# Seven half-size products for the mixing output projection of a hybrid encoder block, with its weight sums made earlier in the program

## What is computed

```
proj = rmsnorm(x) @ w_in            # columns for mLSTM, HGRN2 and the merge gates
y_m, y_h = mlstm(...), hgrn2(...)   # the HGRN2 values come from hg_i, token-major
merged = sigmoid(gate_m) * (y_m @ w_branch_m) + sigmoid(gate_h) * (y_h @ w_branch_h)
x = x + merged @ w_out              # the mixing output projection, 1024x1024 by 1024x1024
u = rmsnorm(x)
q_x = u @ w_q_x                     # cross attention follows, then the gated FFN
```

## Time and profile before

| what | value |
|---|---|
| median of 3 runs | 2567.12 us |
| the profiled execution, its own time | 2570.34 us |
| its span in the trace | 2568.6 us |
| granted TensorE clock, mean | 0.998 |
| PE busy | 2537.1 us (99%) |
| DVE, ACT, POOL busy | 1641.1 (64%), 914.6 (36%), 751.1 (29%) us |
| token-major HGRN projection on PE, first and last start | 478.5 to 565.3 us |
| mixing output projection on PE, with 5 transposes | 1562.42 to 1659.67 us |

### The profile page before, as it was taken

How to read it: one execution, slowest core, us unless ns; L and a number is a source line. 1 busy time by engine, 2 the same in 40 slices (tenths; PEclk the granted TensorE clock), 3 DMA queues, 4 the chain that set the end, 5 groups by cost and what they waited for, 6 DMA issues and landing times. The chain is left out here.

```text
span 2568.6 us, 35010 instructions
## 1 busy us (share of the span) xinstructions
PE 2537.1 (99%) x13888; PEld 2198.3 (86%) x13888; DVE 1641.1 (64%) x1839; ACT 914.6 (36%) x1123; POOL 751.1 (29%) x705
## 2 busy tenths in 40 slices
PE   7999999999999999999999999999999999999998
PEld 7888888889999999998888889977898888888887
DVE  5675555338887888866655424433447998887557
ACT  6342222133343333332324422333233443343433
POOL 2033223002111121235552001167412465553001
PEclk9999999999999999999999999999999999999999
DMA  8323333432323323344444536155414233335755
GB/s 284 117 79 125 106 100 130 136 120 92 103 98 108 103 98 115 107 141 159 159 141 160 168 123 213 34 180 194 159 34 147 74 123 116 106 107 181 280 195 180
DMA packets 184194, 346.49 MB, mean 135 GB/s; under 512 B 10235, under 2 KB 113991, under 8 KB 184032
## 3 DMA queue, kind: packets, MB, share of 16 engines
q1 hardware_dynamic: 122560, 152.34, 18.2%
q0 software_dynamic: 32896, 118.44, 13.4%
q10 hardware_dynamic: 28576, 73.47, 7.8%
HBM read 239.00 MB, written 105.22 MB: 134 GB/s over the span
## 5 line engine op out<-in xcount | busy, mean ns | idle before, releaser
L2273 PE MATMUL ps<-whi,a_hi 128*128 128x256 f32 x1024 | 295.2, 288 | 1.2 <-DVE a_lo L2027 1.1
L2273 PE MATMUL ps<-whi,a_lo 128*128 128x256 f32 x1024 | 289.7, 283 | 0.0
L2273 PE MATMUL ps<-wlo,a_hi 128*128 128x256 f32 x1024 | 289.7, 283 | 0.0
L2242 PE MATMUL ps<-a_hi,whi 128*128 128x512 f32 x608 | 248.1, 408 | 0.2 <-DVE a_lo L1589 0.2
L2242 PE MATMUL ps<-a_hi,wlo 128*128 128x512 f32 x608 | 237.3, 390 | 0.0
L2242 PE MATMUL ps<-a_lo,whi 128*128 128x512 f32 x608 | 236.9, 390 | 0.0
L1570 DVE TENSOR_TENSOR wlo<-raw,whi 128x2048 fp32r<-128x2048 f32 x61 | 141.1, 2312 | 135.8 <-ACT whi L946 135.5
L2273 PEld LDWEIGHTS ps<-whi,a_hi 128*128 128x128 f32 x1024 | 196.4, 192 | 1.9 <-DVE a_lo L2027 1.3
L2273 PEld LDWEIGHTS ps<-wlo,a_hi 128*128 128x128 f32 x1024 | 196.6, 192 | 0.3 <-issue 0.2
L2273 PEld LDWEIGHTS ps<-whi,a_lo 128*128 128x128 f32 x1024 | 196.3, 192 | 0.0
L946 ACT ACTIVATE whi<-raw 128x2048 fp32r<-128x2048 f32 x61 | 116.9, 1916 | 196.4 <-PE ps L2273 111.1
(11 more groups left out here) (402 smaller groups left out, 6610.0 us busy)
## 6 DMA issues: line engine op xcount, KB each, us to landing
raw<-in_w_in SPq DMA_DIRECT2D x45, 1024.0 KB, 6.2
raw<-in_w_up SPq DMA_DIRECT2D x22, 1024.0 KB, 5.2
hg_T<-ev ACTq DMA_DIRECT2D x32, 512.0 KB, 3.0
qfb<-hg_T POOLq DMA_DIRECT2D x24, 512.0 KB, 6.8
wd<-in_w_down POOLq DMA_DIRECT2D x44, 256.0 KB, 3.5
down_weight_sums<-wd POOLq DMA_DIRECT2D x22, 512.0 KB, 4.4
hidden_T<-ga ACTq DMA_DIRECT2D x11, 1024.0 KB, 4.0
hidden_sums<-s POOLq DMA_DIRECT2D x10, 1024.0 KB, 4.7
```

The costliest lines, as they stand in the source:

```text
L2242: ins = pe.matmul(ps[:, u], W[sw][:, b.slot, k, c * P:(c + 1) * P], op[mw][:, k, t * HALF:(t + 1) * HALF], start=k == 0 and q == 0, stop=k ...
L2273: ins = pe.matmul(ps[:, u, part * BC:(part + 1) * BC], op[sw][:, k, t * P:(t + 1) * P], W[mw][:, b.slot, k], start=k == 0 and q == 0, stop ...
```

## The change

The output projection becomes seven products of quarters. A (merged) is cut into a11, a12, a21, a22 by token half and depth half, and w_out into quarters of 4 depth tiles by 512 columns. Each product `out_pe(i)` is 4 token tiles x 4 depths x 3 = 48 matmuls of 128x512, 336 in all. In order they are a11 by b11, a12 by b21, three products of a sum of A's quarters by a sum of w_out's, a sum of A's by b22, and a22 by a sum of w_out's. The four sums of A are made on DVE and split on ACT and DVE while PE works; ACT copies product 0 into a spare part of acc, and DVE adds the products to acc with x.

The four weight sums depend on the weights alone. They are made in eight pieces in the token-major HGRN projection: POOL loads four 128x256 parts of a piece, makes four sums, ACT copies the piece to hi (`out_sum_hi`), POOL subtracts to lo and stores both to memory, 512 KB each. Before it loads the piece after next into the same buffer POOL waits until the stores have landed. In the output projection POOL loads each sum back, 1 MB hi and 1 MB lo, straight into the whi and wlo slots. x comes in four quarters. One `split_lo` on DVE moves ahead of the first head's key products. Cut to its core (renumbered semaphore values and later stages left out):

```diff
@@ sync
-            for b0, name in ((B_OUT, "w_out"), (B_Q, "w_q_x"), (B_O, "w_o_x")):
+            for j in range(2):
+                b = Blk(B_OUT + j)
+                sp.wait_ge(w_lo, b.count(-2))
+                sp.dma_start(wide(raw, b), w_o[:, 4 * j:4 * j + 4, 0:HALF]).then_inc(w_ld[b.slot], 16)
+            b = Blk(B_OUT + 3)
+            sp.wait_ge(w_lo, Blk(B_OUT + 1).count())
+            for j in range(2):
+                sp.dma_start(wide(raw, b)[:, 2 * j:2 * j + 2], w_o[:, 4 + 2 * j:6 + 2 * j, HALF:D]).then_inc(w_ld[Blk(B_OUT + j).slot], 16)
+            weights(Blk(B_Q), wk("w_q_x")[:, :, 0:BC])
@@ gpsimd
+            def out_weights(i):
+                k, h = divmod(i, 2)
+                for kh in range(2):
+                    rows_ = A["w_out"][0][(4 * kh + k) * P:(4 * kh + k + 1) * P, :].rearrange("p (c n) -> p c n", c=2)
+                    pool.dma_start(ow[:, i % 2, 2 * kh:2 * kh + 2], rows_[:, :, h * BC:(h + 1) * BC]).then_inc(a_ld[i % 2], 16)
+            def out_weight_sums(i):
+                k, h = divmod(i, 2)
+                pool.wait_ge(a_ld[i % 2], 32 * (i // 2 + 1))
+                x11, x12, x21, x22_ = [ow[:, i % 2, n] for n in range(4)]
+                line(pool.tensor_tensor(x22_, x22_, x12, ALU.subtract))
+                line(pool.tensor_tensor(x12, x12, x11, ALU.subtract))
+                line(pool.tensor_tensor(x11, x11, x22_, ALU.add))
+                signal(pool, pool.tensor_tensor(x21, x21, x11, ALU.subtract), s_t, OUT_T + i + 1)
+                if i < OUT_PIECES - 1:
+                    if i:
+                        pool.wait_ge(sum_io, 32 * i)
+                    out_weights(i + 1)
+                pool.wait_ge(part_hi, PART0 + i + 1)
+                line(pool.tensor_tensor(ow_lo[:, i % 2], ow[:, i % 2], ow_hi[:, i % 2], ALU.subtract))
+                for n, src in enumerate((ow_hi, ow_lo)):
+                    pool.dma_start(osum_d[n, :, k].rearrange("q p n -> p q n")[:, :, h * BC:(h + 1) * BC], src[:, i % 2]).then_inc(sum_io, 16)
             load_q(0)
+            pool.wait_ge(s_ev, PRODUCTS * N_HS)
+            out_weights(0)
+            for i in range(OUT_PIECES):
+                out_weight_sums(i)
+            pool.wait_ge(sum_io, 32 * OUT_PIECES)
...
+            x_quarter(0, acc[:, 0:4, 0:HALF], 0, 0)
+            pool.wait_ge(*out_done(0, 3))
+            sums_in(0, 0, slot0)
+            pool.wait_ge(*out_done(1, 3))
+            sums_in(1, 3, slot1)
+            x_quarter(1, acc[:, 0:4, HALF:D], 0, 1)
+            x_quarter(2, acc[:, 4:8, 0:HALF], 1, 0)
+            x_quarter(3, x22[:], 1, 1)
+            pool.wait_ge(*out_done(2, 3))
+            sums_in(2, 1, slot0)
+            pool.wait_ge(op_lo, 3 * KT)
+            pool.wait_ge(*out_done(4, 3))
+            sums_in(3, 2, [quarter(t, 0, 1) for t in (a_hi, a_lo)])
@@ scalar
             def pair_act(i, stored):
                 split_hi(b.ahead(1))
+                if i == 0:
+                    for n in range(4):
+                        out_sum_hi(n)
                 split_hi(b.ahead(2), unit_done, b.unit(0))
                 for t in range(NT):
                     pair_out(b, col, t, [v + 16 * (t // 4) for v in stored])
+                    if i == 0 and t in (2, 4, 6, 7):
+                        out_sum_hi(4 + (2, 4, 6, 7).index(t))
@@ vector
             hg_start(0)
+            split_lo(Blk(B_HGN + 3))
             key_products(0, range(2, LEVELS))
             key_sums(0)
-            for j in (2, 3):
-                split_lo(Blk(B_HGN + j + 1))
+            split_lo(Blk(B_HGN + 4))
...
+            out_sum(6, o2[:], a22, s3_, ALU.subtract)
+            out_sum(7, s1_, s1_, a22, ALU.add)
+            quarter_lo(3, s3_, o3_hi[:], o3_lo[:])
+            out_add(0, 0, 1, 2, 3)
+            quarter_lo(4, o2[:], quarter(a_hi, 0, 0), quarter(a_lo, 0, 0))
...
+            for t in range(NT):
+                if t < 4:
+                    out_add(6, t)
+                norm_lo(10 + t, t, a_hi, a_lo)
+                if t in (0, 1, 4, 5, 6):
+                    norm_mul(13 + t - t // 4 * 2, na)
@@ tensor
-            natural(B_OUT, 2 * KT, 10, (range(KT - 2), range(KT - 2, KT)))
+            def out_pe(i, left, right):
+                for t in range(4):
+                    if i == 0:
+                        wait_bank(Blk(B_OUT), t)
+                    elif i >= 2:
+                        pe.wait_ge(*out_taken(i - 2, t))
+                    for k in range(4):
+                        for q, (sw, mw) in enumerate(((0, 0), (0, 1), (1, 0))):
+                            ins = pe.matmul(ps[:, out_bank(i) + t], left[sw][:, k, t * P:(t + 1) * P], right[mw][:, k],
+                                            start=k == 0 and q == 0, stop=k == 3 and q == 2)
...
+                    if i == PRODUCTS - 1:
+                        norm_tr(10 + t, na)
...
+            pe.wait_ge(b_ld[2], 48)
+            pe.wait_ge(op_lo, 2 * KT + 6)
+            out_pe(4, (o1_hi, a21[1]), slot0)
...
+            out_pe(6, a22, a21)
+            norm_tr(14, na)
```

More of the change, by code:

```diff
@@ L330, in build @@
             Sall = sb("Sall", [P, 2, NT, P], F32, c)
+            with ExitStack() as c1:
+                ow_hi = sb("ow_hi", [P, 2, 4, BC], F32R, c1)
             cv = sb("cv", [P, T], F32, c)
@@ L359, in build @@
             acc = sb("acc", [P, NT, D], F32, c)
+            with ExitStack() as c1:
+                o1_hi = sb("o1_hi", [P, 4, HALF], F32R, c1)
+                x22 = sb("x22", [P, 4, HALF], F32, c1)
+                o3_hi, o3_lo = [sb(name, [P, 4, HALF], F32R, c1) for name in ("o3_hi", "o3_lo")]
+                o2 = sb("o2", [P, 4, HALF], F32, c1)
             with ExitStack() as c1:
@@ L480, in combo, with out_done, out_bank, out_taken @@
             return flat[:, o:o + HALF]
+        def out_done(i, t):
+            if t == 3 and i in OUT_SLOT:
+                return unit_done, Blk(B_OUT + OUT_SLOT[i]).unit(3)
+            return prod_done, PART0 + 4 * i + t + 1 - sum(s < i for s in OUT_SLOT)
+        def out_bank(i):
+            return i % 2 * 4
+        def out_taken(i, t):
+            if i in (2, 3, 4):
+                return s_ev, OUT_TAKEN + 4 * (i - 2) + t + 1
+            return res_add, {0: 0, 1: 4, 5: 8, 6: 12}[i] + t + 1
         def down_bank(i, t):
             return 4 * ((i + 1) % 2) + t
+        def merged(t, c):
+            return t[:, KT - 1, 0:HALF] if c else t[:, 4:KT - 1, 0:HALF]
         OUT_TILES = (0, 1, 4, 5, 2, 3, 6, 7)
@@ L1048, in pair_out, with out_sum_hi @@
                                   ev[:, u - 1:u + 1]).then_inc(st[c], 16)
+            def out_sum_hi(i):
+                act.wait_ge(s_t, OUT_T + i + 1)
+                signal(act, act.activation(ow_hi[:, i % 2], ow[:, i % 2], ACT.Copy), part_hi, PART0 + i + 1)
             def pair_act(i, stored):
@@ L1348, in _ @@
                     if n == 7:
[L1349 removed]
+                        for k in (4, 5) if c == 0 else ():
+                            act.wait_ge(a_ld[k], 16)
+                        quarter_hi(1 + c, merged(a_raw, c), merged(a_hi, c))
                     elif n % 2:
@@ L1353, in _ @@
                     q += 1
-            for n in range(4):
-                split_hi(Blk(B_OUT + n + 1))
+            act.wait_ge(s_sum, 5)
+            quarter_hi(3, quarter(a_sum, 0, 1), o3_hi[:])
+            for t in range(4):
+                act.wait_ge(*out_done(0, t))
+                signal(act, act.activation(acc[:, 4 + t, HALF:D], ps[:, t], ACT.Copy), ev_done, Blk(B_OUT).unit(t))
+            act.wait_ge(s_sum, 6)
+            quarter_hi(4, o2[:], quarter(a_hi, 0, 0))
+            act.wait_ge(s_sum, 7)
+            quarter_hi(5, quarter(a_raw, 0, 1), o1_hi[:])
+            quarter_hi(6, quarter(a_raw, 1, 1), quarter(a_hi, 1, 1))
+            act.wait_ge(s_sum, 8)
+            act.wait_ge(*out_done(1, 3))
+            quarter_hi(7, quarter(a_sum, 0, 1), quarter(a_hi, 1, 0))
+            act.wait_ge(*out_done(3, 3))
+            act.wait_ge(w_ld[Blk(B_OUT).slot], Blk(B_OUT + 2).slot_dmas())
+            split_hi(Blk(B_OUT + 3))
+            split_hi(Blk(B_Q))
             def norm_act(w0):
@@ new lines, in _ @@
+            split_lo(Blk(B_OUT + 3))
+            c22 = acc[:, 4:8, HALF:D]
+            dve.wait_ge(x_ld[2], 16)
+            line(dve.tensor_tensor(acc[:, 4:8, 0:HALF], acc[:, 4:8, 0:HALF], c22, ALU.add))
+            dve.wait_ge(x_ld[3], 16)
+            line(dve.tensor_tensor(c22, c22, x22[:], ALU.add))
+            for t in range(4):
+                dve.wait_ge(*out_done(4, t))
+                line(dve.tensor_tensor(acc12[:, t], acc12[:, t], ps[:, t], ALU.add))
+            out_add(4, 0, 1, 2, 3)
```

155 lines of the change are left out of this document (120 added, 35 removed).

## The result

The changed kernel takes 2596.76 us (median of 4 runs, 2595.88 to 2602.82), the kernel before 2568.26 us on the same chip (4 runs). The ratio is 1.0116 with a 95% interval of 1.0099 to 1.0134: slower by 28.5 us. The forecast was 2590.7 us, slower by 23.6.

The account below looks back on a forecast made before the run. The prediction took PE to bound the kernel nearly everywhere. 2570.3 − 12.7 (output projection) + 36.3 (weight sums) = 2593.9 us; with the runs' median 3.2 us lower, it forecast 2590.7 us, range 2577 to 2603.

Parts of the forecast that it names:

- The gain of the matmuls, 16.0 us: Output projection: 768 matmuls of 128x256, 92.2 us, become 336 of 128x512, 76.2 us, taking 16.0 us off PE.
- The 11.4 us: Output projection: alternative matmul gain by the Trainium skill's times, 83.9 − 72.5 us; the prediction kept 16.0.
- What the projection gives back, 3.3 us: Output projection: 0.5 us waiting for product 4's sum and 2.8 us at the closing transposes, making 16.0 into 12.7.
- The pace of POOL: HGRN projection: 9.9 us a piece for the first four, 10.3 for the last four; fourth sum at 527.0, eighth at 568.2.
- Block 2, idle 10.7 us: HGRN projection: block 2, due at 521.8, is ready at 532.4 after copy and splits; PE idles 10.7 us.
- Tiles 5 and 7, 3 and 5 us: HGRN projection, block 2: these tiles wait for the sixth and seventh sums, some 3 and 5 us.
- Block 3, 9.7 us behind the eighth sum, ready at 577.9: HGRN projection: ACT and DVE work after the eighth sum makes block 3, needed at 543.7, 34.2 us late.
- The clock, 2.1 us: HGRN projection: PE's matmuls run at a lower granted clock after the long wait, charged once at 2.1 us.
- the range's lower end: Whole kernel: 2567.1 + 26 − 16 = 2577 us, with pieces of 9.3 us and a first load at 492.
- Rival 1: HGRN projection: pieces come fast enough, the sums are hidden and the change is faster, about 2557 us; chance 0.04.
- Rival 3: Output projection: bound by transfers or DVE, product 4's sum 3.7 us late, gain only 7, about 2596 us; chance 0.15.
- Rivals 2 and 4: HGRN pieces: 2, late stores, 11.5 us each, about 2599, chance 0.2; 4, cheap pieces, 9.3 us, about 2578, chance 0.15.

Follow-up runs that it names:

- second profile of the changed kernel: The changed kernel run once more, unedited, to see how its profiled execution varies: median 2596.51 us, ratio 1.0107 to the kernel before.
- the output projection alone: The changed kernel without the eight pieces of weight sums in the HGRN stage, keeping the seven products: 2556.95 us, ratio 0.9955 to the kernel before.
- the table's last line: The changed kernel with block 3's split ahead of gates and queries on ScalarE and head 0's keys on VectorE: 2593.40 us; its stage takes 119.8 us.
- the run with ScalarE's order changed: The changed kernel with ScalarE's high parts moved to where POOL has them, POOL's part untouched: 2565.82 us, ratio 0.9992 to the kernel before.

## Why the prediction held

The direction, the place and the mechanism were right: the sums are not hidden although their engines are idle, because ScalarE reaches PE's next weights only through POOL's pieces. The measured 28.5 us lie 4.9 us above the forecast, inside the range. By its own steps, with the second profile of the changed kernel:

- **The gain of the matmuls, 16.0 us.** The stretch of 80.80 us holds 336 matmuls and 1.61 us of waiting. 80.8 − 1.6 − 76.2 leaves 3.0 us for the three groups of transposes that stand between the last product's matmuls, about a microsecond each. The term stands. The 11.4 us that the prediction works out from the Trainium skill (TensorE: Matmul & The Clock Gate, "Wait — 56ns, not 53.3ns?") would leave 6.0 after the losses below (1.6 and 3.8), where the output projection alone gained 11.5.
- **What the projection gives back, 3.3 us.** This was too small. Product 4 waited 1.6 us for its sums, not 0.5. At the end the waits of PE from the second group of transposes on are 1.57, 0.57, 1.06 and 1.06 us against 0.17 and 0.29 before:

```profile
1688.93 0.50 PE L2445 MATMUL ps<-a_hi,whi 128*128 128x512 f32 x1 [1.57 <-DVE a_lo L1728]
1692.56 1.09 PE L2495 MATMUL ps<-ident,xn_A 128*128 128x128 f32 x8 [0.57 <-DVE xn_A L1722]
1697.48 1.09 PE L2495 MATMUL ps<-ident,xn_A 128*128 128x128 f32 x8 [1.06 <-DVE xn_A L1722]
1702.39 1.09 PE L2495 MATMUL ps<-ident,xn_A 128*128 128x128 f32 x8 [1.06 <-DVE xn_A L1722]
```

  That is 3.8 us more than before, where I charged 2.8, one group of transposes too few. So 12.7 should have been 10.6, and the measured values are 9.9 by the trace and 11.5 by the run.
- **The pace of POOL.** I had the fourth sum ready at 527.0 us and the eighth at 568.2. ScalarE took them at 527.1 and 567.7, with pieces of 9.4 and then 10.2 us on average against 9.9 and 10.3. That the fourth came to 0.1 us is in part luck: the first was taken at 498.8 where I had 497.3, and the three pieces behind it were 0.5 us shorter each. The 10.2 is a mean too: of the last four pieces one takes 11.8 us and the others 9.5 to 9.7. The reason that I gave, stores that land late when ScalarE and SP store and load too, holds for that one, as POOL shows (the wait for ow_lo's store before a load):

```profile
527.75 1.47 POOL L757 DMA_DIRECT2D ow<-in_w_out  x2 [0.72 <-DMA out_weight_sums<-ow_lo]
...
539.59 1.47 POOL L757 DMA_DIRECT2D ow<-in_w_out  x2 [2.83 <-DMA out_weight_sums<-ow_lo]
...
549.19 1.47 POOL L757 DMA_DIRECT2D ow<-in_w_out  x2 [0.66 <-DMA out_weight_sums<-ow_lo]
```

  SP issues its load of a block at 533.9, ScalarE its stores at 531.4 and 538.6, and from 534 to 539 us 314 GB/s move, against 254 to 262 beside the earlier pieces. In the first profile another load waited 2.50 us, at 522.2, with none of this traffic beside it (178 GB/s from 516 to 522); why that store was late is open.
- **Block 2, idle 10.7 us.** PE waited 12.1 us (14.4 in the first profile). The step that was off is the split's 2.29 us on VectorE. It took 3.5, as POOL's subtraction was under way from 529.24 to 531.59, and it ends 2.2 us after that:

```profile
530.23 3.53 DVE L1709 TENSOR_TENSOR wlo<-raw,whi 128x2048 fp32r<-128x2048 f32 x1 [46.44 <-ACT whi L1050]
```

- **Tiles 5 and 7, 3 and 5 us.** They waited 0.9 and 3.8 us, the first less because block 2 had begun later. Neither counts in the sum, since the next wait is for the eighth piece.
- **Block 3, 9.7 us behind the eighth sum, ready at 577.9.** It was 11.8 us, at 579.6. I had counted the move of `split_lo` ahead of the key products as bringing it straight behind its high part. But `hg_start` still holds fkd, Y and the first two products ahead of it, as the rows of VectorE above show. I had followed ScalarE's queue and not VectorE's; the table's last line is that queue and ScalarE's gates taken away. The delay is 36.2 us from 543.4, not 34.2.
- **The clock, 2.1 us.** Block 3 takes 604.2 − 579.6 = 24.6 us, 2.8 over its 21.8 (24.0 us in the first profile). In the first profile, from 575 to 585 us the granted clock was half of full speed, the lower level, 1.2 GHz, and PE's records there are 0.80 and 0.63 us long instead of 0.39:

```profile
575.00:585.00 10.00, 1.51 (x4) 1.22 (x5) 8.58 (x13) 3.87 (x3) 1.82 (x3) 0.50 0.44 111
585.00:590.00 5.00, 5.00 (x17) 3.99 (x16) 1.18 (x1) 1.26 (x1) 0.00 (x0) 0.70 0.60 203
```

  The loss in block 2 (31.4 us from its first matmul to its last, of which 21.8 are matmuls at full speed and 4.7 waits, which leaves 4.9 of slow clock) disappeared in the wait for the eighth piece, as I had said.

Together the delay of block 3 and the clock are 36.2 + 2.8 = 39.0 us where I had 36.3, and 39.8 by the runs; and about 11 given back where I had 12.7. Of the 4.9 us missed, 2.7 are VectorE's queue before block 3 and the clock, and about 2 the tail and the transfer of product 4.

One bound of the range was added up wrongly. Pieces of 9.3 us and a first load at 492 give a delay of 26.4 us, to which the clock's 2.1 belongs as in the other sums; so the 26 is 28.5, and the range's lower end would have been near 2580, not 2577. With pieces of 11.5 the same sum gives 46, not 45.

Rival 1 (the sums are hidden) fell as an account of this kernel: the pieces took 9.4 to 10.2 us. But its condition, that a piece take under 5.2 us, held only for the order in which the change puts ScalarE's work. With the order changed the sums are hidden at (580.51 − 499.56) / 7 = 11.6 us a piece. I had asked how fast POOL must be, and not whether ScalarE must wait for it. Rival 3 had the right place for 1.6 us but the wrong size. That its 2596 is the measured time is a coincidence: it takes a gain of 7 us and a loss of 36.3, where about 11 and 39.8 were measured. Rivals 2 and 4 would have needed pieces of 11.5 or 9.3 us.

## What to carry to other kernels

Work put on an idle engine costs nothing only if nobody who waits for it has something due queued behind that wait. Before making the helper faster, move the waiting instruction to where the result is already there: here that was worth 37 us, while taking all arithmetic off the helper was worth 9. When such a queue is costed, every engine in the chain has its own order to be read, the last one before PE above all.

## What I had not expected of the hardware

- VectorE and POOL slow each other when both work on SBUF: a subtraction of 128x2048 takes 2.29 us alone and 2.5 to 4.5 beside POOL's arithmetic, a POOL sum of 128x256 takes 0.74 us alone and up to 2.68 beside VectorE's. In the rows of the run with ScalarE's order changed each ends, after the other's instruction is over, within about the time that it takes alone (2.15 and 0.6 us).
- The granted clock also fell after a pause of 3.83 us. In the second profile PE waited from 556.1 to 559.93 us for a copy of tile 7, and its next matmuls ran at the lower level, 1.2 GHz (granted clock 0.50 from 559.9 to 562.0 us, 1.00 from 544 to 549):

```profile
559.93 0.79 PE L2597 MATMUL ps<-whi,a_hi 128*128 128x512 f32 x1 [3.83 <-ACT ev L1149]
560.52 0.63 PE L2597 MATMUL ps<-wlo,a_hi 128*128 128x512 f32 x1
560.95 0.63 PE L2597 MATMUL ps<-whi,a_lo 128*128 128x512 f32 x1
```

  They start 0.43 us apart in place of 0.2267, and the twelve behind the pause take 2.4 us more for it, on top of the 3.83. In the same profile a wait of 0.91 us had no slower matmuls behind it.
